# Half of the second query chunk multiplied inside the first projection stage of a two-layer decoder kernel

## The reference

```python
for l in range(2):
    mod = silu(c) @ w_ada[l] + b_ada[l]          # 6 vectors of 2048
    sh1, sc1, g1, sh2, sc2, g2 = split(mod)
    h = rmsnorm(x, norm_g[l, 0]) * (1 + sc1) + sh1
    u, q, kc, vc, ksl, vsl, kwn, vwn, gl = split(h @ w_in[l])
    a = pool_mixer(u)                            # trailing means, 4 groups
    o = nsa(rmsnorm(q), compressed k/v, selected k/v, window k/v, gates gl)
    x = x + g1 * (concat[a, o] @ w_out[l])
    h2 = rmsnorm(x, norm_g[l, 1]) * (1 + sc2) + sh2
    gate, up = split(h2 @ w_gate_up[l])
    x = x + g2 * ((silu(gate) * up) @ w_down[l])
```

## Time and profile before

| | |
|---|---|
| median of 3 runs | 2160.4 us (2160.2 to 2161.89) |
| the profiled execution, its own time | 2161.69 us |
| its span, first to last instruction | 2159.9 us |
| busy share of the span: PE, DVE, ACT | 98%, 72%, 46% |
| mean DMA rate | 276 GB/s, 595.97 MB |
| granted TensorE clock, mean | 0.995 |

### The profile page before, as it was taken

One profiled execution on the slowest core, in us unless ns is written; L12 is line 12 of the kernel. 1 busy time (PEld: TensorE's weight loads), 2 busy tenths in 40 slices (PEclk: granted clock), 3 DMA queues, 4 the chain that ended last, 5 costly groups with the idle time before them and its releaser, 6 DMA issues.

```text
span 2159.9 us, 25296 instructions
## 1 busy us (share of the span) xinstructions
PE 2124.8 (98%) x9624; PEld 1687.5 (78%) x9624; DVE 1552.1 (72%) x2271; ACT 984.0 (46%) x1515; POOL 208.4 (10%) x392
## 2 busy tenths in 40 slices
PE   7899999999999999999999999999999999999999
PEld 3345888788888888888878788878888888888887
DVE  6767998898688887787877775678755555455555
ACT  2123664744344444443465476475434443344443
POOL 3312122111011111111001100001000000000000
PEclk9999999999999999999999999999999999999999
DMA  9999899899598888888757865468755555555554
GB/s 391 412 393 413 314 341 383 303 349 361 203 340 318 328 320 318 314 317 320 289 205 273 333 242 188 156 230 310 288 215 195 187 186 194 193 191 187 190 192 156
DMA packets 112028, 595.97 MB, mean 276 GB/s; under 512 B 12642, under 2 KB 13090, under 8 KB 65188
## 3 DMA queue, kind: packets, MB, share of 16 engines
q1 hardware_dynamic: 55232, 390.83, 48.4%
q0 software_dynamic: 56384, 203.45, 25.4%
q10 hardware_dynamic: 292, 0.09, 0.0%
HBM read 592.18 MB, written 2.13 MB: 275 GB/s over the span
## 4 chain that ended last, share of the span: by engine, by line
PE 92%; DMA 3%; DVE 2%; issue 2%; ACT 1%; ACTq 0%; DVEq 0%
PE ps L652 80%; PE ps L861 1%; DMA ada<-w_ada 1%; DMA gate<-w_ada 1%; PE ps L1018 1%; PE ps L987 1%; PE ps L1123 1%; DMA kT<-w_ada 1%; PE ps L622 1%; PE ps L621 1%; PE ps L615 1%; PE ps L1064 1%; PE ps L995 1%; PE ps L836 0%; PE ps L790 0%
## 5 line engine op out<-in xcount | busy, mean ns | idle before, releaser
L1651 DVE TENSOR_TENSOR w_lo<-raw,w_hi 128x1024 fp32r<-128x1024 f32 x664 | 799.2, 1223 | 328.3 <-ACT w_hi L1241 327.8
L1241 ACT ACTIVATE w_hi<-raw 128x1024 fp32r<-128x1024 f32 x664 | 694.7, 1058 | 640.7 <-PE ps L652 613.2
L652 PE MATMUL ps<-w_hi,h_hi 128*128 128x512 f32 x1696 | 466.0, 396 | 0.0
L652 PE MATMUL ps<-w_hi,h_lo 128*128 128x512 f32 x1696 | 454.3, 390 | 0.0
L652 PE MATMUL ps<-w_lo,h_hi 128*128 128x512 f32 x1696 | 454.0, 389 | 0.0
L652 PEld LDWEIGHTS ps<-w_hi,h_lo 128*128 128x128 f32 x1696 | 318.3, 188 | 67.6
L652 PEld LDWEIGHTS ps<-w_lo,h_hi 128*128 128x128 f32 x1696 | 318.3, 188 | 67.2
L652 PEld LDWEIGHTS ps<-w_hi,h_hi 128*128 128x128 f32 x1696 | 313.6, 188 | 65.7 <-issue 4.0
L652 PE MATMUL ps<-w_hi,a_hi 128*128 128x512 f32 x848 | 234.4, 398 | 0.0
L652 PE MATMUL ps<-w_hi,a_lo 128*128 128x512 f32 x848 | 227.0, 389 | 0.0
L652 PE MATMUL ps<-w_lo,a_hi 128*128 128x512 f32 x848 | 226.9, 389 | 0.0
(11 more groups left out here) (246 smaller groups left out, 1600.9 us busy)
## 6 DMA issues: line engine op xcount, KB each, us to landing
raw<-stream SPq DMA_DIRECT2D x360, 1024.0 KB, 5.3
ada<-w_ada POOLq DMA_DIRECT2D x182, 512.0 KB, 6.8
qT<-w_ada POOLq DMA_DIRECT2D x52, 512.0 KB, 7.6
uc<-w_ada POOLq DMA_DIRECT2D x29, 512.0 KB, 7.8
kT<-w_ada POOLq DMA_DIRECT2D x26, 512.0 KB, 7.2
val<-w_ada POOLq DMA_DIRECT2D x26, 512.0 KB, 7.5
pT<-w_ada POOLq DMA_DIRECT2D x26, 512.0 KB, 7.5
gate<-w_ada POOLq DMA_DIRECT2D x26, 512.0 KB, 11.7
```

Source lines behind the costliest of these rows:

```text
L652: mm = pe.matmul(banks[tok][0][:], rows[2 * a + k][low][:, tok * P:(tok + 1) * P], w[s][:, k, :], start=first and a == 0 and i == 0 and k ...
L1241: act.activation(whi[h % 4][:].rearrange("p k c -> p (k c)"), raw[t % 4][:, a * 1024:(a + 1) * 1024], ACT.Copy).then_inc(hi_ready.sem, 1)
L1651: dve.tensor_tensor(wlo[h % 4][:].rearrange("p k c -> p (k c)"), raw[t % 4][:, a * 1024:(a + 1) * 1024], whi[h % 4][:].rearrange("p k c -> ...
```

## The change

Half of the second query chunk (8 of its 16 blocks of features) is multiplied early in layer 0. `layer_stream` writes the chunk's four groups of features in the order 2, 0, 1, 3, so tiles 22 and 23 hold groups 0 and 1 (features 0 to 7 of 16). SP loads them into the buffer `gate`, tile 22 behind tile 5 and tile 23 behind tile 8 and the use of the first. PE multiplies them (`early_queries`, 16 matmuls each) into `bank_a` and `bank_b` ahead of the steps of the features 6, 7 and 10, 11. ACT copies the two partial sums at the end of `first_norm` to `q1_part` (the part of `qT` for the second heads), and DVE adds them to the rest of the chunk out of PSUM (`add_parts`, period 25); ACT then squares the sum from SBUF. `first_queries` writes the second stage's order out by hand: tiles 22 and 23 are gone, `hidden(2)` and `hidden(3)` move forward, the first scores stand in the middle of tile 25 and `cmp_out` behind it.

What goes with it: the first 64 halves of `w_ada` have 9 slots instead of 11; slots 9 and 10 are filled only after the early matmuls; `RAW_AFTER` holds tile 9 until 44 sums are done and tile 12 until 62 (60 before); half 64 follows half 63 in slot 0. `ROOM` takes 9 sums out of the periods 12 to 22 (1, 2, 1, 2, 1 and 2) and puts one more each into 26, 27, 28, 38, 40, 42, 44, 45 and 47. In layer 1 the order of the groups of features differs, and two scratch places (`bufb` and the other half of `qT`).

```diff
--- before.py
+++ after.py
@@ -61,7 +61,8 @@
 UNSPLIT = half_of(T_U0)
-RAW_AFTER = {1: 6, 2: 8, 3: 14, 12: 60}
+RAW_AFTER = {1: 6, 2: 8, 3: 14, 9: 44, 12: 62}
+Q1_GROUPS, Q1_EARLY, EARLY_BEHIND = (2, 0, 1, 3), (22, 23), (5, 8)
 HALVES = half_of(TILES)
@@ -150,7 +151,7 @@
 ADA_K = D // 2
-ADA_RING, ADA_SLOTS = 3, 11
+ADA_RING, ADA_SLOTS, FIRST_SLOTS = 3, 11, 9
@@ -180,8 +181,8 @@
 ATT_SPLIT = [t for t in range(10, T_MLP) if t not in DIRECT]
-ROOM = ({10: 3, 11: 2, 12: 5, 15: 5, 17: 4, 18: 4, 20: 2, 22: 2, 25: 2, 26: 3, 27: 1, 28: 2, 29: 4, 30: 3,
-         31: 4, 33: 4, 34: 3, 35: 3, 36: 4, 38: 1, 39: 4, 40: 2, 41: 3, 42: 2, 43: 3, 44: 1, 45: 2, 47: 2, 49: 2} |
+ROOM = ({10: 3, 11: 2, 12: 4, 15: 3, 17: 3, 18: 2, 20: 1, 25: 2, 26: 4, 27: 2, 28: 3, 29: 4, 30: 3, 31: 4, 33: 4, 34: 3, 35: 3,
+         36: 4, 38: 2, 39: 4, 40: 3, 41: 3, 42: 3, 43: 3, 44: 2, 45: 3, 47: 3, 49: 2} |
         {T_MLP + j: n for j, n in ((0, 1), (1, 1), (2, 2), (3, 2), (4, 1), (5, 2), (6, 2), (7, 2), (8, 1))},
@@ -228,7 +229,7 @@
         if q < FIRST_HALVES:
-            s = q % ADA_SLOTS
+            s = q % FIRST_SLOTS
         else:
...
@@ -391,6 +393,8 @@
         nmax, sums, fac = sb("nmax", [P, 2, 2]), sb("sums", [P, 2, 2]), sb("fac", [P, 2, 2])
+        q1_part = [qT[:, tok, 4:8].rearrange("p h t -> p (h t)") for tok in range(TOKS)]
...
@@ -486,7 +492,18 @@
             flat = stream.rearrange("l t p c -> (l t) p c")
+            def load_early(i):
+                if i:
+                    sp.wait_ge(q1_used.sem, 1)
+                sp.dma_start(gate[:], flat[Q1_EARLY[i]]).then_inc(q1_landed.sem, 16)
             def load(n):
+                if n in (*Q1_EARLY, T_Q1[3]):
+                    if n != Q1_EARLY[0]:
+                        return
+                    n = T_Q1[3]
                 s, cols = n % 4, tile_cols(n % TILES)
@@ -520,6 +537,8 @@
                         load(layer * TILES + t + 4)
+                    if layer == 0 and t + 4 in EARLY_BEHIND:
+                        load_early(EARLY_BEHIND.index(t + 4))
                     for d in FREED_LATE.get(t, ()):
@@ -549,6 +568,8 @@
                     pool.wait_ge(ada_summed.sem, before + 1)
+                elif s in (9, 10):
+                    pool.wait_ge(q1_used.sem, 2)
                 pool.dma_start(ada_buf[s], w_ada[q]).then_inc(ada_landed[s].sem, 16)
@@ -745,22 +766,25 @@
-            def unsplit(t, banks, g, between):
+            def unsplit(t, banks, g, between, first=0):
...
                         bank, free, value = banks[tok]
-                        if g == 0 and a == 0:
+                        if g == first and a == 0:
...
                                            raw[t % 4][:, (2 * a + k) * COLS:(2 * a + k + 1) * COLS],
-                                           start=(kt == 0), stop=(kt == KT - 1))
-                        if a == 0 or g == 3:
+                                           start=(kt == 4 * first), stop=(kt == KT - 1))
+                        if t == T_Q1[3] and (a, tok) == (0, 0):
+                            mm.then_inc(gemm_done.sem, 9)
+                        elif a == 0 or g == 3:
                             mm.then_inc(gemm_done.sem, 1)
@@ -840,10 +864,55 @@
+            def early_queries(h):
+                pe.wait_ge(q1_landed.sem, 16 * (h + 1))
+                for tok, (bank, uses) in enumerate(((bank_a, A_USE), (bank_b, B_USE))):
+                    if h == 0:
+                        pe.wait_ge(bank.free.sem, bank.free.at(here, uses["kv 0"]))
+                    for i in range(4):
+                        mm = pe.matmul(bank.tile[:], xT[:, 4 * h + i, tok * P:(tok + 1) * P],
+                                       gate[:, i * COLS:(i + 1) * COLS],
+                                       start=(h == 0 and i == 0), stop=(h == 1 and i == 3))
+                mm.then_inc(q1_used.sem, 1)
+            def skip_landed(t):
+                loaded(t)
+                pe.sem_inc(raw_landed[t % 4].sem, 16)
+            def first_queries():
+                def q0(t):
+                    unsplit(t, chunk(C_Q), T_Q0.index(t), lambda: middle(t))
+                q0(12)
+                gate_logits()
+                kv_turn(1)
+                hidden(0)
+                q0(15)
+                kv_turn(2)
+                hidden(1)
+                q0(17)
+                skip_landed(T_CMP1[2])
+                hidden(2)
+                skip_landed(T_Q0[3])
+                q0(18)
+                hidden(3)
+                unsplit(T_Q1[0], chunk(C_Q + 1), Q1_GROUPS[0], lambda: None, Q1_GROUPS[0])
+                hidden_fold()
+                stage_turn(bank_a, A_USE["q 0"], ST_Q0, 0, 4)
+                stage_turn(bank_b, B_USE["q 0"], ST_Q0 + 1, 1, 4)
+                unsplit(T_Q1[3], chunk(C_Q + 1), Q1_GROUPS[3], lambda: attention_side(25), Q1_GROUPS[0])
+                cmp_out()
             def first_chunks(chunks):
...
                 for ks in steps:
+                    if ks[0] in (6, 10):
+                        early_queries((ks[0] - 6) // 4)
                     for i, banks in enumerate(chunks):
@@ -883,6 +952,8 @@
                         pe.wait_ge(chunk_free[b].sem, chunk_free[b].at(here, C_KV // 2 + 1))
+                        if here.layer == 0:
+                            pe.wait_ge(q1_kept.sem, 2)
                         stage_turn(bank, uses["kv 0"], None, tok, 4, qT[:, tok].rearrange("p h t -> p (h t)"))
...
@@ -1167,17 +1238,17 @@
                     norm(1, T_KV, chunks)
-                for i, t in enumerate((*T_Q0, *T_Q1)):
+                if layer == 0:
+                    first_queries()
+                for i, t in enumerate((*T_Q0, *T_Q1) if layer else ()):
                     if t == 23:
...
                     g = i % 4
-                    if layer == 0:
-                        unsplit(t, chunk(C_Q + i // 4), g, lambda t=t: middle(t))
-                    else:
-                        tile(t, chunk(C_Q + i // 4), h_rows(g), g == 0, g == 3, lambda t=t: middle(t))
+                    tile(t, chunk(C_Q + i // 4), h_rows(g if i < 4 else Q1_GROUPS[g]), g == 0, g == 3,
+                         lambda t=t: middle(t))
                     if t == 12:
...
@@ -1369,6 +1441,10 @@
                         .then_inc(norm_hi.sem, 1)
+                act.wait_ge(q1_used.sem, 2)
+                act.wait_ge(ada_summed.sem, QUERIES_FREE)
+                for tok, bank in enumerate((bank_a, bank_b)):
+                    act.activation(q1_part[tok], bank.tile[:], ACT.Copy).then_inc(q1_kept.sem, 1)
                 act.sem_inc(norm_staged.sem, 8)
@@ -1459,9 +1535,9 @@
                     copy_chunk(T_Q0[3], C_Q, lambda tok: bufb[:, tok, :],
-                               lambda tok: qT[:, tok, 4:8].rearrange("p h t -> p (h t)"))
+                               lambda tok: qT[:, tok, 0:4].rearrange("p h t -> p (h t)"))
                     if here.layer == 0:
-                        act.sem_inc(raw_free[T_Q0[3] % 4].sem, 1)
+                        act.sem_inc(raw_free[T_Q0[3] % 4].sem, 2)
                 if t == 22:
@@ -1475,10 +1551,15 @@
                          cv[:, CV["k_gain"]:CV["k_gain"] + 1])
-                if t == 26:
+                if t == 26 and here.layer:
                     copy_chunk(25, C_Q + 1, lambda tok: bufb[:, tok, :], lambda tok: uc[:, tok * 512:(tok + 1) * 512])
-                    if here.layer == 0:
-                        act.sem_inc(raw_free[T_Q1[3] % 4].sem, 1)
+                if t == 26 and here.layer == 0:
+                    for tok in range(TOKS):
+                        b = chunk_bank(C_Q + 1, tok)
+                        act.wait_ge(chunk_free[b].sem, chunk_free[b].at(here, (C_Q + 1) // 2 + 1))
+                        square_heads(bufb[:, tok], ss, tok, REP, uc[:, tok * 512:(tok + 1) * 512])\
+                            .then_inc(q1_squared.sem, 1)
+                    act.sem_inc(raw_free[T_Q1[3] % 4].sem, 1)
                 if 1 <= m <= NSTEP:
@@ -1861,7 +1942,18 @@
+            def add_parts():
+                dve.wait_ge(q1_kept.sem, 2)
+                for tok in range(TOKS):
+                    b = chunk_bank(C_Q + 1, tok)
+                    dve.wait_ge(gemm_done.sem, gemm_done.at(here, 2 * half_of(T_Q1[3]) + 2 + tok + 1))
+                    dve.tensor_tensor(bufb[:, tok, :], ps[b][:], q1_part[tok], ALU.add)\
+                        .then_inc(chunk_free[b].sem, 1)
             def stage_rstd(c, n):
+                if here.layer == 0 and c == C_Q + 1:
+                    dve.wait_ge(q1_squared.sem, 2)
                 for tok in range(TOKS):
...
@@ -2090,6 +2182,8 @@
                     silu_hidden()
+                if t == 25 and here.layer == 0:
+                    add_parts()
                 if t == 25:
@@ -2214,7 +2308,7 @@
     for first in (1024, 1536, 0, 512):
-        chunk(w_in, first, every)
+        chunk(w_in, first, [4 * g + i for g in Q1_GROUPS for i in range(4)] if first == 1536 else every)
```

16 lines of the change are left out of this document (10 added, 6 removed).

## The result

The changed kernel takes **2172.57 us** in the median (2171.44 to 2175.09), the kernel before 2161.05 on the same chip. The ratio is 1.0055, with a 95% interval from 1.0043 to 1.0066: 11.5 us slower, where 5 us faster was forecast. The profiled execution itself took 2172.85 us (span 2171.1), that of before 2161.69.

What follows compares the result with a forecast made beforehand. PE bounds the kernel, the first stage hangs on bytes, DVE is second bound behind the second stage. 4.7 - 13.9 + 3.4 + 0.5 + 0.3 = -5.0 us from median 2160.4 gives 2155.4 us; range 2150.5 to 2161.5.

Steps and rivals of the forecast that it cites:

- Step 1: Second stage: two tiles of 16 matmuls removed take 13.9 us off PE's path.
- step 6: Tile 26 and attention steps: later tile and DVE's added work take back 3.4 us, periods 27 and 28 about 0.5 more.
- Step 2: First stage, PE: 13.9 us added, 4.9 back from the clock; 9.0 us growth fits pauses of 10.7 us.
- Step 3: First stage, bytes: last feature 5.7 us later, second stage begins 4.7 us later (bounds 2.5 and 8).
- Steps 4 and 5: ACT's two copies hidden, DVE's additions 1.28 us not hidden; SP's queue makes no stall, at most 1 us.
- Step 7: Sums moved to period 38 and later: 0.3 us lost at period 40, nothing in 42 to 47, at most 2.
- D: Rival, attention steps from tile 25 on: sums and additions overload DVE, slower, 2165.5 us; chance 0.09.
- C: Rival, first stage: early tiles land after the features are ready, 13.9 us only moved, 2160.5 us; chance 0.09.

Runs made afterwards that it cites:

- e1: Changed kernel with all nine moved sums of w_ada back in periods 12 to 22; 2171.25 us (ratio 1.0046).
- e16: Changed kernel with eleven slots, tiles 10 and 11 held, and all nine sums where they were before the change; 2164.57 us (ratio 1.0014).
- e7: Changed kernel with only 2 of the 16 matmuls in each early lot, all DMAs as changed; 2171.39 us (ratio 1.0047).
- e8: Changed kernel with a quarter of each early tile loaded and multiplied four times over; 2165.81 us (ratio 1.0022).
- e13: Changed kernel with tile 26 asked for ahead of tile 24 in SP's order; 2167.76 us (ratio 1.0030).
- e5: Changed kernel with eleven slots again for the first 64 halves; 2172.26 us (ratio 1.0049).
- e11: Changed kernel with eleven slots, and tiles 10 and 11 held until 52 and 54 sums are done; 2166.48 us (ratio 1.0025).
- e3: Kernel before with nine slots instead of eleven for the first 64 halves; 2167.11 us (ratio 1.0027).
- e2: Kernel before with nothing but the sums dealt anew; 2170.12 us (ratio 1.0038).
- e9: Changed kernel with only a quarter of each of the halves 133 to 143 loaded, DVE's work as it was; 2167.00 us (ratio 1.0026).
- e12: Changed kernel with eleven slots, tiles 10 and 11 held, and five of the nine moved sums put back; 2159.83 us (ratio 0.9992).
- e15: Changed kernel with five of the nine moved sums put back, nine slots, nothing held; 2164.87 us (ratio 1.0017).
- e10: Changed kernel with halves 133 to 143 loaded in full but three quarters of their sums left out; 2170.07 us (ratio 1.0037).

## Why the prediction was wrong, step by step

The prediction's sum was -5.0, the profile shows +11.3 at tile 52. By stretches (measured less forecast) the difference of 16.3 us is: first stage 10.4 - 4.7 = 5.7, second stage 13.9 - 9.6 = 4.3, tiles 26 to 30 4.7 - 3.9 = 0.8, tiles 30 to 42 0.3 as forecast, late 5.6 where nothing was forecast. So three steps failed: PE's pauses together with the order of arrival (2 and 3), and the late sums (7). The prediction named a start of the second stage later than 142 as a sign that it is wrong; it was 145.03.

*Step 1, second stage.* PE did lose 13.9 us of work, but the stage got only 9.6 shorter: 3.94 us are the wait for tile 26 at its end (step 6). That these 13.9 us are worth their length at all holds only with sums taken out, which e1 and e16 show: the stage is bound by bytes just as by PE. DVE had waited 20.3 us for w_ada there before the change already (13.5 and 6.8), nearly all of the 21.4 us that I called idle. The row that said so stood in the prediction, "PE full and the DMA full (1.01)", and I used its first half only.

*Step 2, PE's pauses: the step that failed first.* I set 9.0 us of work against pauses of 10.7 us as they were before. The pauses are made by the arrival of features, and the added bytes and the missing slots move the arrival: the pair 6, 7 came 4.2 us later, 10, 11 4.1, 12, 13 11.4. So the pauses opened again, one behind the added work and one before the features 12, 13. By the medians e7 and e8 show it from both sides. Of the clock's 4.9 us little more than 1 came back: 1.7 are lost behind the 7.27 us pause, and 12 matmuls behind the wait for tile 26 took 5 us, where they took 2.9 in e13.

*Step 3, bytes.* The last feature's scaling was forecast to end at 132.6 and ended at 133.5, so the sum of bytes was nearly right, with some luck: it began at 132.9 here and at 132.5 to 135.8 in the other executions with the same instructions. The place was wrong. I let the last feature alone decide and had 8 us of work follow it. The pair 12, 13 decided, with 44 matmuls and the turns behind it (121.64 to 145.03). Its halves were asked for 6.6 to 6.9 us later, by the nine slots and by sums that were late themselves, and the tiles 10 and 11 only 1.0 us later, so that these no longer came behind half 55 but with it; holding them is worth 5.8 us (e5 against e11). The slots alone cost 3.8 us at the second stage in e3 where I had 2.1 less a reserve. Repaired together (e11), the second stage begins 3.1 us later than before the change, under the 4.7 forecast. Eleven slots alone gave nothing (e5), so the share of the slots here is not one number.

The prediction quoted the Trainium skill ("DMA: Bandwidth & Descriptors", section "Queues, rings and completion order") that each engine takes packets in turn from the queues with work, and counted it as in the sum already. It wasn't: the halves 54 and 55 took 15.2 and 17.4 us from issue to landing with tiles among them, against 12.8 and 12.4. The trace agrees with the rule, in a place where the order decides.

*Steps 4 and 5* held. ACT's two copies ran at 134.08 for 1.07 us behind the last scaling, with PE at work until 142 on matmuls already begun, and PE waited for no raw tile of the second stage; tile 25 landed at 187.1, 2 us ahead of its use.

*Step 6, tile 26.* Issued at 188.46 where I had 182.4, which is mostly the 5.7 us of the first stage; landed after 9.6 us where I took 6.2 and had 7.8 as the heavy end. Tile 27 was asked for right behind it and shared the queue. The mechanism (the tile waits for tile 20's buffer in SP's order) was right, as e13 shows. I had seen it as DVE's chain from w_lo, and that held too: from the first w_lo (199.17) to the third step's bias (217.12) it took 17.95 us where I had 18.2, and the third step's turn came 3.1 behind it where I had 3.0. It began 9.5 us late, so the turn was at 220.23 instead of 210.9. What I hadn't seen is the wait of 3.94 us before the first turn, which came through ACT's exp behind the split. The tiles 26 to 30 took 4.7 us more, where I had 3.4 and 0.5.

*Step 7, the late sums: the second step that failed.* Nothing was forecast behind period 40, with 2 as the most; 5.6 came, and 7.0 in e2. I compared the added sums with DVE's idle time, 4.2 us. Each sum is also a request: out of the second stage, nine sums took their requests along, and the DMA there ran at 371 instead of 413 GB/s (in e2, where no tile was moved, at 361); put where the DMA is full (share 0.96 to 1.04 from 296 to 375) they waited, and at tile 42 four halves more than before were still to come. e9 shows that bytes have most of it, e12 and e15 that it goes when five sums go back. My rows had the DMA share in both places.

*The rivals.* D had the sign and the place of a part, with 2165.5; its mechanism, DVE's work uncovered, is the lesser part (3.1 of 5.6 us in e10). C did not come, but it was near: the early tiles took 13.0 and 11.6 us to land, not 7.8, and the first was there at 65.34, 0.4 us before PE took it up. No rival had the first stage lose more than 8 us, and none had the late stretch hang on the DMA. What decides is the balance: the forecast weighed PE alone where PE, DVE and DMA were full together.

## What to carry to other kernels

A pause of an engine in a stage that is bound by transfers is not free room: work that brings bytes along moves every later arrival, so lay out the arrival of each input anew, and not only of the last one. And where a buffer ring asks for the next transfer when the last is consumed, moving a consumer moves its transfer too: read the DMA's share both where work is taken out (there the DMA goes idle) and where it is put in. If several resources are full in the same stretch, as here, relieving one gave next to nothing (e1) before the bytes were dealt anew, and then only up to the balance: all nine sums moved gave 2166.5, four moved 2159.8, none moved 2164.6 with everything else alike.

## What the runs showed of the hardware

The first stage with nine slots is not the same from one execution to the next. The second stage began at 140.3 to 146.8 us in six profiled executions that have the same instructions up to there (the changed kernel, e1, e9, e10, e13, e15), and at 137.1 to 139.0 in six with eleven slots and held tiles. In three of the kernels with nine slots the features 4, 5 came at 62 to 63 us, in the others at 54.6 to 58.2. The rows of e3 above show the edge: halves that come 3.8 us apart (56.88, 60.66, 64.43), where the halves 50 to 54 of the same run, with no tile on its way, land 1.2 to 1.3 us apart (105.4 to 110.6); at the time of those rows SP's tiles 4 to 6 are on their way.
